# Layer boundary of a two-layer decoder kernel: when the next weights are sent, how wide the small projection's operand is, and halves in the last LayerNorm

## What is computed

```python
for i in range(2):
    proj = h @ w_in[i]                   # 1024 -> fox qkv, f(8) | pool | gdn qkv, b(4), a(4), z | gates
    mix  = merge(forgetting_attention(...), multiscale_pool(...), gated_deltanet(...), gates) @ w_out[i]
    h    = layer_norm(alpha * h + mix, ln1)
    q    = h @ w_q[i]                    # 8 heads, product keys, top 16 of 128^2 experts
    idx, wts = topk(q, sub_k1, sub_k2)   # (256, 8 x 16)
    act  = gelu(sum(u_tab[idx] * h)) * wts
    ffn  = sum(act * v_tab[idx])         # 128 gathered rows for each token
    ple  = sigmoid(h @ ple_gate[i]) * (p[i] @ ple_proj[i])
    h    = layer_norm(alpha * h + ffn + ple, ln2)
```

## Time and profile before

| | |
|---|---|
| median of 3 runs | 1999.05 us (1998.58 to 1999.45) |
| the profiled execution's own time | 2000.26 us |
| its span in the profile | 1998.3 us |
| busy: PE, DVE, ACT, POOL | 1769.2, 1374.9, 918.1, 681.4 us |
| moved by DMA | 660.57 MB, mean 331 GB/s |
| mean granted TensorE clock | 0.987 |

### The profile page before, as it was taken

How to read it: one execution, slowest core, us unless ns; L and a number is a source line. 1 busy time by engine, 2 the same in 40 slices (tenths; PEclk the granted TensorE clock), 3 DMA queues, 4 the chain that set the end, 5 groups by cost and what they waited for, 6 DMA issues and landing times.

```text
span 1998.3 us, 26336 instructions
## 1 busy us (share of the span) xinstructions
PE 1769.2 (89%) x7336; PEld 1025.8 (51%) x7336; DVE 1374.9 (69%) x3480; ACT 918.1 (46%) x2233; POOL 681.4 (34%) x583
## 2 busy tenths in 40 slices
PE   8989998999999887888799899999989998787876
PEld 7877777554434322222288778775544342232222
DVE  5774466877767777776468655668777677777764
ACT  5545442544444444444355454415445344444443
POOL 0100001344434465655401100014443344556553
PEclk9999999999999999999999999999999999999999
DMA  6532458999999999999944234689999999999997
GB/s 239 167 103 85 137 171 315 425 425 426 425 426 377 423 426 426 427 427 426 421 151 162 86 106 139 198 322 425 426 425 426 426 384 427 425 427 426 425 425 296
DMA packets 106584, 660.57 MB, mean 331 GB/s; under 512 B 11872, under 2 KB 12272, under 8 KB 39920
## 3 DMA queue, kind: packets, MB, share of 16 engines
q0 software_dynamic: 75376, 546.57, 65.6%
q1 hardware_dynamic: 31104, 112.71, 17.0%
HBM read 658.17 MB, written 1.06 MB: 330 GB/s over the span
## 4 chain that ended last, share of the span: by engine, by line
PE 40%; DMA 28%; DVE 13%; issue 8%; ACT 7%; POOL 3%; DVEq 0%; POOLq 0%; ACTq 0%; SPq 0%
DMA arena<-experts_dram,stage 13%; DMA arena<-experts_dram,idxu 11%; PE acc L719 11%; PE psum L639 5%; PE psum L640 5%; PE psum L641 5%; PE acc L738 4%; DMA cst<-experts_dram,stage 3%; DVE arena L1520 2%; PE psum L700 2%; PE psum L668 2%; DVE arena L1464 2%; ACT w_hi_r L1040 2%; DVE raw_r L1374 1%; DMA cst<-experts_dram,idxu 1%
## 5 line engine op out<-in xcount | busy, mean ns | idle before, releaser
L738 PE MATMUL acc<-arena 128*128 128x512 f32 x896 | 443.5, 623 | 119.2 <-ACT arena L1134 111.6
L719 PE MATMUL acc<-arena 128*128 128x512 f32 x896 | 416.1, 604 | 35.7 <-ACT arena L1108 35.4
L1494 DVE CUSTOM_DVE_ANT_0 arena<-arena,h 128x1024 f32<-128x1024 f32 x224 | 274.4, 1225 | 144.1 <-DMA arena<-experts_dram,stage 67.4
L605 POOL DMA_INDIRECT arena<-experts_dram,stage x224 | 295.1, 1318 | 215.5 <-PE acc L738 137.9
L738 PEld LDWEIGHTS acc<-arena 128*128 128x128 f32 x896 | 158.2, 193 | 403.6 <-issue 403.1
L1464 DVE CUSTOM_DVE_ANT_0 arena<-arena,h 128x1024 f32<-128x1024 f32 x224 | 274.4, 1225 | 129.9 <-DMA arena<-experts_dram,idxu 125.7
L587 POOL DMA_INDIRECT arena<-experts_dram,idxu x224 | 244.9, 1093 | 341.5 <-PE acc L719 300.5
L719 PEld LDWEIGHTS acc<-arena 128*128 128x128 f32 x896 | 162.1, 190 | 270.7 <-issue 151.7
L1374 DVE TENSOR_TENSOR raw_r<-raw,w_hi_r 128x1024 fp32r<-128x1024 f32 x152 | 180.0, 1220 | 125.0 <-ACT w_hi_r L1040 124.3
L1040 ACT ACTIVATE w_hi_r<-raw 128x1024 fp32r<-128x1024 f32 x152 | 153.9, 1053 | 72.4 <-DMA raw<-weights_dram 54.2
L1128 ACT ACTIVATE gel<-dots 128x1 f32<-128x1 f32 x256 | 51.9, 203 | 294.1 <-DVE dots L1494 293.5
(11 more groups left out here) (295 smaller groups left out, 2793.5 us busy)
## 6 DMA issues: line engine op xcount, KB each, us to landing
raw<-weights_dram SPq DMA_DIRECT2D x184, 512.0 KB
w_hi<-weights_dram SPq DMA_DIRECT2D x12, 512.0 KB, 8.9
lnr<-lnrows_dram POOLq DMA_DIRECT2D x4, 1024.0 KB, 6.7
arena<-weights_dram SPq DMA_DIRECT2D x8, 512.0 KB, 5.3
arena<-experts_dram,idxu POOLq DMA_INDIRECT x224
arena<-experts_dram,stage POOLq DMA_INDIRECT x224
lnr<-cum_dram POOLq DMA_DIRECT2D x2, 1024.0 KB, 8.9
cst<-consts_dram SPq DMA_DIRECT2D x1, 1448.0 KB, 12.1
```

Of the source, the lines that this page charges most:

```text
L605: nc.gpsimd.indirect_dma_start(slots[i % RING][:, :], None, experts[:, :], bass.IndirectOffsetOnAxis(stage[:, i:i + 1], 0)).then_inc(slot_ ...
L719: last = mm(acc[:, c * 512:(c + 1) * 512], diag[:, i % 4, :], slots[n % RING][:, D + c * 512:D + (c + 1) * 512], start=False, stop=n == RA ...
L738: last = mm(acc[:, c * 512:(c + 1) * 512], diag[:, i % 4, :], slots[i % RING][:, D + c * 512:D + (c + 1) * 512], start=False, stop=ends)
L1494: nc.vector.tensor_tensor_reduce(slots[i % RING][:, 0:D], slots[i % RING][:, 0:D], h[:, b, :], 1.0, 0.0, ALU.mult, ALU.add, dots[:, i:i + ...
```

## The change

- SP's wait before layer 1's first weight becomes one for the landing of the last gathered row of layer 0. POOL's wait before it loads the next parameters goes. ACT and DVE split all four pieces of a layer's first group at the step ("smallT",) in both layers, and nothing at ("ln2", 1).
- `w_small` gets 112 more columns, filled once from the parameter block, so that PE can take 128 columns from any k-tile's start as the left operand. The product then fills 128 rows of the bank; rows 0 to 15 are read, as before.
- The statistics of the second block's last LayerNorm, in both layers, start with the first half of the accumulator when that half is filled (a new semaphore from PE), and wait for the other half only before the second `bn_stats`.
- In the very last LayerNorm the final operation is done in two halves of 512 columns, and SP sends each half when it is ready.

```diff
@@ first_group, SP
-        def last_rows(L):
-            return row_used, RING + (L + 1) * NB * RANKS - 4
-                    sp.wait_ge(*last_rows(L - 1))
+                    sp.wait_ge(*landed(L - 1, NB * RANKS - 1))
-            for b in range(NB):
-                sp.wait_ge(h2_ready, (DEPTH - 1) * NB + b + 1)
-                sp.dma_start(out[b * P:(b + 1) * P, :], h[:, b, :]).then_inc(out_sent, 16)
-            sp.wait_ge(out_sent, 16 * NB)
+            sp.wait_ge(h2_ready, (DEPTH - 1) * NB + 1)
+            sp.dma_start(out[0:P, :], h[:, 0, :]).then_inc(out_sent, 16)
+            sp.wait_ge(h2_half, 1)
+            sp.dma_start(out[P:T, 0:512], h[:, 1, 0:512]).then_inc(out_sent, 16)
+            sp.wait_ge(h2_ready, DEPTH * NB)
+            sp.dma_start(out[P:T, 512:D], h[:, 1, 512:D]).then_inc(out_sent, 16)
+            sp.wait_ge(out_sent, 16 * 3)
@@ POOL, ("ln2", 1)
-                        pool.wait_ge(*last_rows(L))
                         pool.dma_start(par[:, :], params[L + 1]).then_inc(params_in, 16)
@@ PE
+                                if ends and c == 0:
+                                    last.then_inc(acc_half, 1)
+                        pe.wait_ge(small_pad_ready, 1)
-                            last = mm3(ps[0:16, 0:T], [w_small[:, i2, k * 16:(k + 1) * 16] for i2 in range(2)], ...)
+                            last = mm3(ps[:, 0:T], [w_small_all[:, i2 * P + k * 16:][:, 0:P] for i2 in range(2)], ...)
@@ ACT
+                        if L == 0:
+                            AC(w_small_all[:, 2 * P:3 * P - 16], par[:, Q_WS:Q_WS + P - 16], ACT.Copy).then_inc(small_pad_ready, 1)
                     if step == ("smallT",):
-                        for piece in first_group(L)[2 if L else 0:]:
-                            split_hi(*piece)
-                    if step == ("ln2", 1):
-                        for piece in first_group(L + 1)[0:2]:
+                        for piece in first_group(L):
                             split_hi(*piece)
@@ DVE
-            def statistics(src):
+            def statistics(src, whole=None):
                 nc.vector.bn_stats(bst[:, 0:6], src[:, 0:512])
+                if whole:
+                    dve.wait_ge(*whole)
                 link(nc.vector.bn_stats(bst[:, 6:12], src[:, 512:1024]))
-                STT(h[:, b, :], r, rstd[:, 0:1], lnr[:, D:2 * D], ALU.mult, ALU.add).then_inc(ready, 1)
+                if n == 4 * DEPTH:
+                    STT(h[:, b, 0:512], r[:, 0:512], ...).then_inc(h2_half, 1)
+                    STT(h[:, b, 512:D], r[:, 512:D], ...).then_inc(ready, 1)
+                else:
+                    STT(h[:, b, :], r, rstd[:, 0:1], lnr[:, D:2 * D], ALU.mult, ALU.add).then_inc(ready, 1)
-                        for piece in first_group(L)[1 if L else 0:]:
-                    if step == ("ln2", 1):
-                        for piece in first_group(L + 1)[0:1]:
+                        for piece in first_group(L):
                             split_lo(*piece)
@@ DVE, ln2, second block
-                            layer_norm(acc[:, :], base[:, 1, :], 1, L * 4 + 4, h2_ready)
+                            dve.wait_ge(acc_half, L + 1)
+                            for part in (statistics(acc, (acc_filled, NB * (L + 1))), norm(acc[:, :], base[:, 1, :], 1, L * 4 + 4, h2_ready)):
```

More of the change, by code:

```diff
@@ L265, in build @@
         hT = hidden_r.rearrange("p (i k t) -> p i k t", i=2, k=KT)
-        w_small = sb("w_small", 2 * KT * 16, F32R).rearrange("p (i n) -> p i n", i=2)
+        w_small_all = sb("w_small", 3 * KT * 16 - 16, F32R)
+        w_small = w_small_all[:, 0:2 * KT * 16].rearrange("p (i n) -> p i n", i=2)
         arena, arena_r = two_ways("arena", 25612)
@@ L385, in build @@
         w_lo_ready = sem("w_lo_ready")
-        act_hi_ready, small_hi_ready, small_lo_ready = (sem(n) for n in ("act_hi_ready", "small_hi_ready", "small_lo_ready"))
+        act_hi_ready, small_hi_ready, small_lo_ready, small_pad_ready = (sem(n) for n in ("act_hi_ready", "small_hi_ready", "small_lo_ready", "small_pad_ready"))
         bank_filled = [sem(f"bank_filled{i}") for i in range(NBANK)]
@@ L404, in build @@
         acc_filled, acc_drained, base_ready = sem("acc_filled"), sem("acc_drained"), sem("base_ready")
+        acc_half, h2_half = sem("acc_half"), sem("h2_half")
         def gate_of(n, c, b):
@@ L484, in split_at @@
             return [(L, piece) for piece in SPLIT_AT.get(step, ())]
-        def last_rows(L):
-            return row_used, RING + (L + 1) * NB * RANKS - 4
         def first_group(L):
-            return [(L, (0, j)) for j in range(len(GROUPS[0][2]))] if L < DEPTH else []
+            return [(L, (0, j)) for j in range(len(GROUPS[0][2]))]
         HI_STEPS = [st for st in FILLS if st[0] in ("hT", "mT", "poolmix", "foT", "oT")]
@@ L811, in _ @@
                         for k in range(KT):
-                            last = mm3(ps[0:16, 0:T], [w_small[:, i2, k * 16:(k + 1) * 16] for i2 in range(2)], [hT[:, i2, k, :] for i2 in range(2)], k == 0, k == KT - 1)
+                            last = mm3(ps[:, 0:T], [w_small_all[:, i2 * P + k * 16:][:, 0:P] for i2 in range(2)], [hT[:, i2, k, :] for i2 in range(2)], k == 0, k == KT - 1)
                     elif kind == "small":
@@ L1363, in norm @@
                 dve.wait_ge(rstd_ready, n)
-                STT(h[:, b, :], r, rstd[:, 0:1], lnr[:, D:2 * D], ALU.mult, ALU.add).then_inc(ready, 1)
[L1366 to L1369, removed]
+                if n == 4 * DEPTH:
+                    STT(h[:, b, 0:512], r[:, 0:512], rstd[:, 0:1], lnr[:, D:D + 512], ALU.mult, ALU.add).then_inc(h2_half, 1)
+                    STT(h[:, b, 512:D], r[:, 512:D], rstd[:, 0:1], lnr[:, D + 512:2 * D], ALU.mult, ALU.add).then_inc(ready, 1)
+                else:
+                    STT(h[:, b, :], r, rstd[:, 0:1], lnr[:, D:2 * D], ALU.mult, ALU.add).then_inc(ready, 1)
             def split_lo(L, piece):
@@ L1382, in _ @@
                     if step == ("smallT",):
-                        for piece in first_group(L)[1 if L else 0:]:
-                            split_lo(*piece)
-                    if step == ("ln2", 1):
-                        for piece in first_group(L + 1)[0:1]:
+                        for piece in first_group(L):
                             split_lo(*piece)
@@ L1437, in _ @@
                         dve.wait_ge(ln_in, 16 * (2 * L + 2))
-                        dve.wait_ge(acc_filled, L * NB + b + 1)
                         if b:
-                            layer_norm(acc[:, :], base[:, 1, :], 1, L * 4 + 4, h2_ready)
+                            dve.wait_ge(acc_half, L + 1)
+                            for part in (statistics(acc, (acc_filled, NB * (L + 1))), norm(acc[:, :], base[:, 1, :], 1, L * 4 + 4, h2_ready)):
+                                for _ in part:
+                                    pass
                             continue
+                        dve.wait_ge(acc_filled, L * NB + 1)
                         dve.wait_ge(base_ready, L * NB + 1)
```

## The result

The changed kernel takes 2010.9 us, the median of four runs (2007.39 to 2015.34), against 1998.82 (1997.84 to 1999.45) for the kernel before on the same chip: ratio 1.0056 [1.0042, 1.007], slower by more than the 0.2% that a measurement can tell. The forecast was 1996.4, the range 1993.0 to 1998.1. The profiled execution took 2007.39, its span is 2005.6 us.

What follows compares the result with a forecast made beforehand. The prediction took the layer boundary after the last gathered row to be serial, with PE gapless from the small projection. Terms -0.79 - 1.22 - 0.60 + 0 = -2.6 took the median 1999.05 to 1996.4 us, range 1993.0 to 1998.1.

Steps and rivals of the forecast that it cites:

- part 4: Small projection, 128-column operand from the wider w_small: clock sets matmul time, loads overlap, extra ACT copy hidden; 0.
- The bounds of that step: Small projection's 128-column operand: loads show, +0.08 x 24 = +1.9 us a layer, or the clock rises sooner.
- Step 1: Layer boundary: weights leave after the last gathered row lands, last dots about 2.46 apart; -0.79 us, later weights hidden.
- Step 2: Second block's last LayerNorm, each layer: statistics by halves, second half starts 0.1 after PE's end; -0.61 each, -1.22 us.
- its first rival: Small projection: clock rises sooner, 1993.0 us, chance 0.22; if the rise stays at 1009.76, 0.7 of the gain goes.
- a microsecond won before or inside the small projection is worth a microsecond: Layer boundary: PE runs without a gap from the small projection to gdn0, so time won counts fully until something else is late.
- Step 3: End of the kernel, output by halves: +0.01 for two final operations, -0.62 for the shorter tail; term -0.60 us.
- Its bound of 0: Output by halves: the low end of its bounds, 0 to -0.8 us, where a fixed transfer cost dominates.
- Step 4: Small projection with 128 columns: 24 matmuls 0.21 apart cold, 0.12 warm, clock rise 4.6 to 5 us in; 0.
- The slow rival: Small projection at 1.2 GHz: matmuls wait for 0.29 us loads, +3.8, 2000.2 us; chance 0.06 together with late weights.
- the fast one: Small projection: wide operand or new moment lifts the clock within 2 to 3 us; 3.4 us more, 1993.0; chance 0.22.
- the sign: Small projection: expected evidence for the forecast, the clock rising 4.6 to 5 us into the 24 matmuls.

Runs made afterwards that it cites:

- c3: The changed kernel with w_small rounded up from 368 to 384 columns, every gather slot's offset past a multiple of 256 as before: 1999.44 us, ratio 0.9999.
- a1: The kernel before with 112 unused columns (448 bytes) ahead of the arena, giving it the changed kernel's layout: 2015.12 us, ratio 1.0078.
- a4: The kernel before with unused columns and moved slots so that all eight gather slots start on multiples of 256 bytes: 1994.47 us, ratio 0.9972.
- b2: a4 with all eight slots 64 bytes past a multiple of 256: 2011.18 us in one execution, the kernel before 2004.21 on that chip.
- b3: a4 with all eight slots 128 bytes past a multiple of 256: 2011.31 us in one execution, the kernel before 2004.21 on that chip.
- b1: a4 with all eight slots 32 bytes past a multiple of 256: 2013.45 us in one execution, the kernel before 2004.21 on that chip.
- b4: a4 with all eight slots 224 bytes past a multiple of 256: 2017.84 us in one execution, the kernel before 2004.21 on that chip.

## Why the prediction was wrong

- **The failed step is part 4's cost, and in it a term that the sum did not have.** The part was costed as an operand, a load and a copy ("I take 0"), and the layout that its 112 columns shift was no term. The bounds of that step (+1.9 a layer) were about TensorE, too; the row stages, 1280 of 2000 us and bound by DMA, were taken as untouched. They cost +11.2 us (1.2 + 4.4 + 1.6 + 4.0), +14.4 beside c3, and +13.5 in a1 with no other change. The layout could be read before: an allocation ahead of the destination of 512 gathers grew by 448 bytes, and 448 is no multiple of 256. That a start off a multiple costs anything could have been bounded from the profile of before, in the medians by slot above: 2.410 to 2.450 for slots 0 to 3, 2.470 to 2.490 for slots 4 to 7, on average 0.043 apart. On half of 512 rows that is 11 us. That it meets the 11.2 is in part luck: the medians are block 0's, and in block 1, where the cost fell for the most part, they show nothing.
- **Step 1, right.** The last dots are 2.46 apart (-0.79), ACT waits for no weight before piece 7, the parameters behind the last gather cost nothing that shows.
- **Step 2, right at its place** (-0.68 in each layer against -0.61), wrong in what reached the end. The text had it in its first rival: if the rise stays while PE starts earlier, half of the gain goes. The rise came 16.84 after the last dot, before 16.47, so 0.23 of 0.82 was left at the freed slot and nothing behind the piece that fills it. That "a microsecond won before or inside the small projection is worth a microsecond" did not hold.
- **Step 3, mis-sized**: -0.60, measured -0.16 for the tail behind the last issue and +0.13 for the halves, so nothing. Its bound of 0 ("fixed cost dominates") was the case: half the bytes, yet 2.84 of 3.0 us remain.
- **Step 4, right as far as it went.** 0.21 apart cold with 128 columns; the first matmul of the group is 0.18 slower (0.55 and 0.35 to the next, the kernel before 0.37 and 0.17). The slow rival (0.29 apart) and the fast one (clock up at 2 to 3 us) both fell; in layer 1 the rise came 5.76 us into the group and the matmuls behind it, later than the 4.6 to 5 that were given as the sign.
- What the rows after the change give for the four parts is -0.79 for the last dot, nothing to -0.23 behind it and -0.7 at the end: -1.5 to -1.7 us, not -2.6, and the timed kernels without the shift lie within 3 us of zero. So the gains are seen where they were forecast, and they are about a seventh of what the shift cost.

The clock and the loads got the attention because the rivals were looked for inside the edited steps. The one with the right sign was in the edit's declaration.

## To carry to other kernels

When an edit changes the size of an on-chip array, list the arrays allocated behind it and see which of them transfers land in; pad so that the destinations of large transfers start at a multiple of 256 bytes. In a stage that DMA fills, the GB/s of a plateau is the number to compare first: it told 421 from 426 with one execution each, where the totals wandered by more. A short serial piece won before the clock has risen is given back in part if the rise does not move with it.

## What the runs showed of the hardware

A gather that writes 8192 bytes into each partition costs about 1.5% more when the destination starts off a multiple of 256 bytes: with all eight slots alike 2.446 us a row on it (a4), 2.482 and 2.483 for 64 and 128 bytes past (b2, b3), 2.491 and 2.490 for 32 and 224 (b1, b4); 427 against 420 to 422 GB/s, 309.1 against 313.8 to 314.8 ns for a packet of 8192 bytes. The edits move arrays on the chip alone; the table that the rows are read from stays. The Trainium skill ("DMA: Bandwidth & Descriptors", "How a descriptor splits into AXI transactions") says, of reading, that a transaction must start from a 256-byte-aligned address, and that a descriptor which doesn't start on one has its first transaction begin at the boundary below, with the unused bytes still costing beats. By that account 8192 bytes have 33 transactions instead of 32 and, at 32 bytes to a beat, 1 beat more of 256 at an offset of 32 and 7 at 224, an estimate of 0.4% and 2.7%. Here it is the address written to that moves. The runs agree in the boundary and in the sign; they do not agree that it grows with the offset, 1.8% at both.

Two transfers of 256 KB to the output, issued 0.66 us apart, landed 2.0 and 2.4 us after their issues, one of 512 KB 2.6; halving the last one took 0.16 off the end.
